# Residual stream turned on VectorE in 32x32 blocks, with block-wise DMAs and a DRAM scratch, instead of by TensorE transposes

## The reference

```
h = rmsnorm(x, norm_mix_g);  z = h @ w_in + b_in      # gates, three mixers A, B, C
mix = sig(ga)*(A @ w_br_a) + sig(gb)*(B @ w_br_b) + sig(gc)*(C @ w_br_c)
x = x + mix @ w_o                                     # first residual sum, "x2"
h2 = rmsnorm(x, norm_ffn_g)
u, v = split(h2 @ w_up);  u = causal_dwconv(u, ffn_conv_w)   # 2816 channels each
x = x + (silu(u) * v) @ w_down                        # second residual sum
return rmsnorm(x, norm_final_g)
```

## Time and profile before

| | |
|---|---|
| three timed runs | 939.05, 939.93, 939.99 us; median 939.93 |
| the profiled execution | 939.24 us, of which span 937.5 us |
| granted PE clock over the span | 0.998 |
| busy | PE 918.0, DVE 495.9, ACT 378.3, POOL 377.4 us |
| DMA | 87.61 MB in 149234 packets, mean 93 GB/s |

### The profile page before, as it was taken

One profiled execution on the slowest core, in us unless ns is written; L12 is line 12 of the kernel. 1 busy time (PEld: TensorE's weight loads), 2 busy tenths in 40 slices (PEclk: granted clock), 3 DMA queues, 4 the chain that ended last, 5 costly groups with the idle time before them and its releaser, 6 DMA issues.

```text
span 937.5 us, 13783 instructions
## 1 busy us (share of the span) xinstructions
PE 918.0 (98%) x4488; PEld 761.0 (81%) x4488; DVE 495.9 (53%) x957; ACT 378.3 (40%) x655; POOL 377.4 (40%) x195
## 2 busy tenths in 40 slices
PE   6999999998999999999999999999999999999997
PEld 5888888887788888888888888888888888888885
DVE  4326464566565645656547687666666666400004
ACT  6445354353444543554533336333333333311125
POOL 4454444442233423324234443444444444444441
PEclk9999999999999999999999999999999999999999
DMA  6353434332122222222253232333333333322232
GB/s 184 94 150 101 108 101 107 105 90 68 46 68 55 81 69 68 70 63 67 67 158 104 76 90 81 99 89 105 97 89 97 105 89 100 124 90 90 90 112 90
DMA packets 149234, 87.61 MB, mean 93 GB/s; under 512 B 24767, under 2 KB 139853, under 8 KB 149205
## 3 DMA queue, kind: packets, MB, share of 16 engines
q1 hardware_dynamic: 149205, 87.23, 32.3%
HBM read 85.09 MB, written 2.11 MB: 93 GB/s over the span
## 4 chain that ended last, share of the span: by engine, by line
PE 94%; DVE 3%; ACT 1%; POOL 1%; DMA 1%; issue 0%; SPq 0%; DVEq 0%; POOLq 0%; ACTq 0%
PE z_bank L647 23%; PE z_bank L649 23%; PE z_bank L648 23%; PE s_bank L647 3%; PE s_bank L648 3%; PE s_bank L649 3%; PE s_bank L683 3%; PE s_bank L703 3%; PE o_bank L722 1%; PE o_bank L647 1%; PE o_bank L723 1%; PE s_bank L723 1%; PE s_bank L722 1%; PE o_bank L649 1%; PE o_bank L648 1%; DMA x_in<-in_x 1%
## 5 line engine op out<-in xcount | busy, mean ns | idle before, releaser
L554 POOL TENSOR_TENSOR w_lo<-raw,w_hi 128x1024 fp32r<-128x1024 f32 (+1 forms) x144 | 352.5, 2448 | 527.1 <-ACT w_hi L967 430.5
L647 PE MATMUL z_bank<-h_hi,w_hi 128*128 128x512 f32 x768 | 302.2, 393 | 0.0
L649 PE MATMUL z_bank<-h_hi,w_lo 128*128 128x512 f32 x768 | 299.6, 390 | 0.0
L648 PE MATMUL z_bank<-h_lo,w_hi 128*128 128x512 f32 x768 | 299.3, 390 | 0.0
L967 ACT ACTIVATE w_hi<-raw 128x1024 fp32r<-128x1024 f32 x117 | 123.4, 1054 | 181.2 <-PE z_bank L649 181.2
L647 PEld LDWEIGHTS z_bank<-h_hi,w_hi 128*128 128x128 f32 x768 | 144.3, 188 | 30.6 <-POOL w_lo L554 0.5
L649 PEld LDWEIGHTS z_bank<-h_hi,w_lo 128*128 128x128 f32 x768 | 144.2, 188 | 30.4
L648 PEld LDWEIGHTS z_bank<-h_lo,w_hi 128*128 128x128 f32 x768 | 144.3, 188 | 28.9
L1570 DVE SCALAR_TENSOR_TENSOR u_c<-u_t,cols,u_c 128x512 f32<-128x512 f32 x44 | 65.8, 1496 | 25.2 <-ACT u_c L1194 22.1
L976 ACT ACTIVATE p_f<-p_f,neg_mx 128x128 f32<-128x128 f32 (+1 forms) x96 | 52.6, 550 | 45.1 <-DVE neg_mx L1438 29.5
L1585 DVE TENSOR_TENSOR y_out<-s_bank,x_t 128x512 f32<-128x512 f32 x5 | 3.5, 691 | 110.4 <-PE s_bank L649 110.3
(11 more groups left out here) (316 smaller groups left out, 1328.3 us busy)
## 6 DMA issues: line engine op xcount, KB each, us to landing
raw<-in_w_in SPq DMA_DIRECT2D x112, 256.0 KB, 3.2
raw<-in_w_up SPq DMA_DIRECT2D x88, 256.0 KB, 3.1
raw<-in_w_down SPq DMA_DIRECT2D x42, 256.0 KB, 2.9
raw<-in_w_o SPq DMA_DIRECT2D x16, 256.0 KB, 3.2
x_in<-in_x SPq DMA_DIRECT2D x4, 512.0 KB, 5.2
f_bias<-cum_scratch SPq DMA_DIRECT2D x4, 512.0 KB, 4.4
raw<-in_w_br_a SPq DMA_DIRECT2D x8, 256.0 KB, 3.0
raw<-in_w_br_b SPq DMA_DIRECT2D x8, 256.0 KB, 3.3
```

The costliest lines, as they stand in the source:

```text
L554: pool.tensor_tensor(w_lo[:, slot, 0:wide], raw[:, slot, 0:wide], w_hi[:, slot, 0:wide].bitcast(F), ALU.subtract) \
L647: pe.matmul(out, w[0], r[0], start=first, stop=False)
L648: pe.matmul(out, w[0], r[1], start=False, stop=False)
L649: return pe.matmul(out, w[1], r[0], start=False, stop=last)
```

## The change

- PE's 32 transposes of `x_r` and 32 of `x2` are gone, with ACT's 8 copies out of PSUM for the first and 8 for the second.
- x is loaded block-wise: four DMAs, each into 32 partitions, each of 4096 pieces of 32 floats (128 B) that stand 512 B apart in DRAM. In `x_b`, partition 32a+j holds, for its 16 tokens, the pieces a of all channel tiles. One DVE instruction per channel tile (`dve.transpose`, on 16 blocks of 32x32) turns them into `x2[:, m, :]`. It reads runs of 32 floats and writes single floats 16 apart.
- After `h_lo`, DVE turns x2 the other way into `x2_b` (single floats 16 apart read, runs of 32 written). SP stores `x2_b` in four DMAs of 4096 pieces of 128 B into a DRAM scratch, behind the loads of UP5, and reads it back as rows in four DMAs of 512 KB into `x2_t`, behind the loads of UP11.
- The squares move from DVE to ACT, between `h_hi` and the next `split_hi`. Their running sum moves from DVE to POOL, behind the `split_lo` of tile m+2.

```diff
@@ buffers
-            x_r = sb("x_r", [P128, QT, D_MODEL], F, s)
+            x_b = sb("x_b", [P128, QT * D_MODEL], F, s)
...
+            x2_b = sb("x2_b", [P128, QT * D_MODEL], F, s)
...
-        x_sq = sb("x_sq", [P128, SEQ], F, ffn)
+        x_sq = sb("x_sq", [P128, 2, SEQ], F, ffn)
@@ SP
-                    for t in range(QT):
-                        sp.dma_start(x_r[:, t, :], x_v[:, t, :]).then_inc(xr_loaded, 16)
+                    by_block = x[0].rearrange("t c -> (t c)").rearrange("(j n a i) -> a j n i", j=BLK, n=P128, a=4)
+                    for a in range(4):
+                        sp.dma_start(x_b[BLK * a:BLK * a + BLK, :].rearrange("p (n i) -> p n i", i=BLK), by_block[a]) \
+                            .then_inc(xb_loaded, 16)
...
-            with sp.Fori(0, FT) as i:
+            for i in range(3):
+                load_up(i)
+            sp.wait_ge(x2_turned, KT)
+            by_block = x2_dram.rearrange("t c -> (t c)").rearrange("(j n a i) -> a j n i", j=BLK, n=P128, a=4)
+            for a in range(4):
+                sp.dma_start(by_block[a], x2_b[BLK * a:BLK * a + BLK, :].rearrange("p (n i) -> p n i", i=BLK)).then_inc(x2_stored, 16)
+            for i in range(3, 6):
+                load_up(i)
+            sp.wait_ge(x2_stored, 16 * 4)
+            for t in range(QT):
+                sp.dma_start(x2_t[:, t, :], x2_dram.rearrange("(t p) n -> p t n", p=P128)[:, t, :]).then_inc(x2_loaded, 16)
+            with sp.Fori(6, FT) as i:
+                load_up(i)
@@ POOL
+            for m in range(KT):
+                split_lo((N_WO + m + 2) % 2, N_WO + m + 2)
+                if m:
+                    pool.wait_ge(sq_done, m + 1)
+                    pool.wait_ge(acc_done, m - 1)
+                    pool.tensor_tensor(x_acc[:, :], x_acc[:, :], x_sq[:, m % 2, :], ALU.add).then_inc(acc_done, 1)
@@ PE
-            pe.wait_ge(xr_loaded, 16 * QT)
             for m in range(KT):
-                if m >= 4:
-                    pe.wait_ge(xr_copied, m - 3)
-                for t in range(QT):
-                    mm = pe.transpose(S[m % 4][:, P128 * t:P128 * t + P128], x_r[:, t, P128 * m:P128 * m + P128], ident[:, :])
-                mm.then_inc(xr_t, 1)
...
-            pe.wait_ge(acc_done, KT)
+            pe.wait_ge(acc_done, KT - 1)
             pe.matmul(S[4][:, :], ones[:, :], x_acc[:, :], start=True, stop=True).then_inc(ss_done, 1)
...
-            pe.wait_ge(xr_copied, KT)
-            turn_x2(0)
             project(0, 1, N_UP + 1, Z_UP[1])
-            pe.wait_ge(x2_kept, QT)
-            turn_x2(1)
@@ ACT
-                act.wait_ge(xr_t, m + 1)
-                act.activation(x2[:, m, :], S[m % 4][:, :], ACT.Copy).then_inc(xr_copied, 1)
...
+                if m > 2:
+                    act.wait_ge(acc_done, m - 2)
+                act.activation(x_sq[:, m % 2, :] if m else x_acc[:, :], x2[:, m, :], ACT.Square).then_inc(sq_done, 1)
@@ DVE
+                if m == 0:
+                    dve.wait_ge(xb_loaded, 16 * 4)
+                dve.transpose(x2[:, m, :].rearrange("p (j b) -> p b j", j=BLK),
+                              x_b[:, :].rearrange("p (b m i) -> p m b i", m=KT, i=BLK)[:, m, :, :]).then_inc(xb_turned, 1)
...
-                sq = x_sq if m else x_acc
-                dve.tensor_tensor(sq[:, :], x2[:, m, :], x2[:, m, :], ALU.mult).then_inc(sq_done if m else acc_done, 1)
-                if m:
-                    dve.wait_ge(sq_done, m)
-                    dve.tensor_tensor(x_acc[:, :], x_acc[:, :], x_sq[:, :], ALU.add).then_inc(acc_done, 1)
+                dve.transpose(x2_b[:, :].rearrange("p (b m i) -> p m b i", m=KT, i=BLK)[:, m, :, :],
+                              x2[:, m, :].rearrange("p (j b) -> p b j", j=BLK)).then_inc(x2_turned, 1)
...
+            dve.wait_ge(x2_loaded, 16 * QT)
```

More of the change, by code:

```diff
@@ L98 @@
 MIX_ORDER = (("gc", 6), ("yc", 0), ("yc", 2), ("gc", 7), ("yc", 4), ("yc", 6))
+BLK = 32
 N_BLK = SEQ // CMP_STRIDE
@@ L255, in hybrid_block @@
         with ExitStack() as s:
-            x_r = sb("x_r", [P128, QT, D_MODEL], F, s)
+            x_b = sb("x_b", [P128, QT * D_MODEL], F, s)
         act_hi = sb("act_hi", [P128, FT, SEQ], R, ffn)
+        with ExitStack() as s:
+            act_lo_ahead = sb("act_lo_ahead", [P128, FT - KT, SEQ], R, s)
+            x2_b = sb("x2_b", [P128, QT * D_MODEL], F, s)
         act_lo = sb("act_lo", [P128, FT, SEQ], R, ffn)
-        x_sq = sb("x_sq", [P128, SEQ], F, ffn)
+        x_sq = sb("x_sq", [P128, 2, SEQ], F, ffn)
         x_acc = sb("x_acc", [P128, SEQ], F, ffn)
@@ L271, in hybrid_block @@
         banks = [*S, O, *Z]
+        x2_dram = nc.dram_tensor("x2_scratch", [SEQ, D_MODEL], F, kind="Internal").ap()
         cum_dram = nc.dram_tensor("cum_scratch", [FOX_HEADS, SEQ], F, kind="Internal").ap()
@@ L330, in hybrid_block @@
         mix_hi = sem("mix_hi"); mix_lo = sem("mix_lo")
-        xr_loaded = sem("xr_loaded"); xr_t = sem("xr_t"); xr_copied = sem("xr_copied");
+        xb_loaded = sem("xb_loaded"); xb_turned = sem("xb_turned")
         xg_hi = sem("xg_hi"); xg_lo = sem("xg_lo"); sq_done = sem("sq_done"); acc_done = sem("acc_done")
@@ L335, in hybrid_block @@
         uv_done = sem("uv_done"); act_hi_done = sem("act_hi_done"); act_lo_done = sem("act_lo_done")
-        down_done = sem("down_done"); x2_turned = sem("x2_turned"); x2_kept = sem("x2_kept")
+        down_done = sem("down_done"); x2_turned = sem("x2_turned"); x2_stored = sem("x2_stored"); x2_loaded = sem("x2_loaded")
         last_loaded = sem("last_loaded"); last_hi_done = sem("last_hi_done"); last_lo_done = sem("last_lo_done")
@@ L521, in _, with load_up @@
                 n += 1
-            with sp.Fori(0, FT) as i:
+            def load_up(i):
                 load8(N_UP + 2 * i, 1, up_k, P128 * i)
                 load8(N_UP + 2 * i + 1, 0, up_k, D_FF + P128 * i)
+            for i in range(3):
[11 more added lines that the diff above has]
+                load_up(i)
             def load_down(n, slot, j):
@@ L634, in _ @@
                                base=SEQ - P128, pattern=[[0, 2], [-1, SEQ]], channel_multiplier=1).then_inc(alibi_ready, 1)
-            with pool.Fori(0, (N_END - 1 - N_NSA - 2) // 2) as i:
+            with pool.Fori(0, (N_WO - N_NSA - 2) // 2) as i:
                 split_lo(1, N_NSA + 2 * i + 2)
                 split_lo(0, N_NSA + 2 * i + 3)
+            split_lo(N_WO % 2, N_WO)
+            split_lo((N_WO + 1) % 2, N_WO + 1)
+            for m in range(KT):
[4 more added lines that the diff above has]
+                    pool.tensor_tensor(x_acc[:, :], x_acc[:, :], x_sq[:, m % 2, :], ALU.add).then_inc(acc_done, 1)
+            with pool.Fori(0, (N_END - 1 - N_UP - 2) // 2) as i:
+                split_lo(1, N_UP + 2 * i + 2)
+                split_lo(0, N_UP + 2 * i + 3)
             pool.wait_ge(last_hi_done, 1)
@@ L926, in down @@
                 return mm3(banks[2 * t + h][:, :], (act_hi[:, j, toks], act_lo[:, j, toks]), (whi[:, cols], wlo[:, cols]), first, last)
-            pe.wait_ge(x2_kept, 2 * QT)
             for j in range(FT - 2):
@@ L1179, in _ @@
             act.activation(rstd[:, :], S[4][:, :], ACT.Sqrt, bias=eps_c[:, :], scale=1.0 / D_MODEL).then_inc(rs_sqrt, 1)
[L1181 to L1186, removed]
             act.activation(act_cell[:, 3:4], eps_c[:, :], ACT.Silu)
@@ L1199, in up_pair @@
                 act.activation(act_hi[:, i, :], u_c[:, :], ACT.Copy).then_inc(act_hi_done, 1)
-            up_pair(0)
-            keep_x2(1)
-            with act.Fori(1, FT) as i:
+            with act.Fori(0, FT) as i:
                 up_pair(i)
@@ L1541, in _ @@
                 z = m % 2
-                dve.wait_ge(xr_copied, m + 1)
+                if m == 0:
+                    dve.wait_ge(xb_loaded, 16 * 4)
+                dve.transpose(x2[:, m, :].rearrange("p (j b) -> p b j", j=BLK),
+                              x_b[:, :].rearrange("p (b m i) -> p m b i", m=KT, i=BLK)[:, m, :, :]).then_inc(xb_turned, 1)
+                dve.wait_ge(xb_turned, m + 1)
                 dve.wait_ge(tile_done, T_WO + m + 1)
@@ L1548, in _ @@
                                          ALU.mult, ALU.subtract).then_inc(xg_lo, 1)
-                if m:
-                    dve.wait_ge(acc_done, m)
-                sq = x_sq if m else x_acc
-                dve.tensor_tensor(sq[:, :], x2[:, m, :], x2[:, m, :], ALU.mult).then_inc(sq_done if m else acc_done, 1)
-                if m:
-                    dve.wait_ge(sq_done, m)
-                    dve.tensor_tensor(x_acc[:, :], x_acc[:, :], x_sq[:, :], ALU.add).then_inc(acc_done, 1)
+                dve.transpose(x2_b[:, :].rearrange("p (b m i) -> p m b i", m=KT, i=BLK)[:, m, :, :],
+                              x2[:, m, :].rearrange("p (j b) -> p b j", j=BLK)).then_inc(x2_turned, 1)
             dve.memset(u_t[:, 0:2], 0.0).then_inc(rs_ready, 1)
```

## The result

| | before | after |
|---|---|---|
| median, us | 939.49 (938.67 to 939.99, 4 runs) | 959.93 (958.9 to 961.02, 4 runs) |
| profiled execution, us | 939.24 | 958.9 |
| its span, us | 937.5 | 957.2 |
| mean granted clock of TensorE | 0.998 | 0.987 |

After is slower by 2.2%: the ratio is 1.022, with an interval of 1.0206 to 1.0233. The forecast was 941.1 in a range of 936 to 952, so the time lies outside it, on the side that the forecast called the likelier.

The account below looks back on a forecast made before the run. PE was taken as the bound, 94% of the chain that ended last. From the profiled 939.24: minus 3.8 won on PE, plus 1.3 for the load of x, plus 4.4 for the store of x2, gives 941.1 us; range 936 to 952.

Parts of the forecast that it names:

- what leaves PE: Transposes gone from the WO tiles and behind the ones matmul: 6.8 us taken off PE, 3.8 us won in all.
- T: Start of the ones matmul, from which later tiles are counted; predicted at 567.7, against 569.12 before.
- The two DVE instructions that I took at 1.5: Ahead of the first pair's silu, before UP3's weight split: 1.5 us predicted with POOL idle, against 2.90 before.
- rival 5: DVE becomes the bound in the WO tiles if a transpose takes 2.78 us: 17 us lost, 958; chance 0.08.
- I take 11.5, between the line and the count: Load of x: ns per 128 B packet, between 9.4 (line through 256 and 512 B) and 14.1 (packets alone count).
- rival 3: Block transfers: packets count, 12.7 to 14.1 ns each or a little more, 943.5 to 947 us; chance 0.17.
- Rival 4: Store of x2: 128 B writes to DRAM cost double, S = 23.6, stall at UP6 16.2 us, 952.9; chance 0.15.
- X: Duration of the block load of x ahead of gc 7's weights: 11.8 us predicted (9.6 to 14.4).
- S: Duration of the block store of x2 ahead of UP6's weights: 11.8 us predicted, costing 4.4 us (2.2 to 7.0).
- landing must be by 494.2: X up to 10.5 costs nothing: gc 7's weights, wanted at 498.05 less the splits' 1.14 + 2.54; X = 11.8 costs 1.3 us (0 to 3.9).
- 483.7 + X: Predicted landing of gc 7's weights: issue at 480.87, 0.9 and 0.4 us of delays, 1.5 us for 512 KB, plus X.
- the formula: At UP6: weights land at T+18.2+S, due at T+25.6, so 7.4 us are free; S = 11.8 costs 4.4 us.

Follow-up runs that it names:

- Run 9: Changed kernel with both block transfers in 4 KB pieces, each DMA over all 128 partitions instead of 32; 936.02 us, ratio 0.9963 to the kernel before.
- run 11: Changed kernel with both block transfers in 256 B pieces, each DMA over all 128 partitions instead of 32; 945.65 us, ratio 1.0073 to the kernel before.
- run 4: Changed kernel with ACT's two copies to `br_hi` ahead of the split of the next weights in the branch steps, instead of behind it; 956.79 us.
- run 6: Changed kernel with both block transfers in 4 KB pieces instead of 128 B, still 32 partitions per DMA; 950.20 us.
- run 12: Changed kernel with both block transfers in 4 KB pieces, each DMA over 64 partitions; 946.93 us, ratio 1.0088 to the kernel before.
- run 10: Changed kernel, pieces still 128 B, but each DMA over all 128 partitions instead of 32; 959.11 us, ratio 1.021 to the kernel before.
- run 3: Changed kernel with block loads spread over three places of SP's program and one weight load behind each block store; 937.29 us, ratio 0.9978 to the kernel before.

## Why the prediction was wrong

**Right in mechanism and nearly in size: what leaves PE.** From the first matmul of WO0 to the ones matmul are 53.36 us, against 54.31 before: 0.95 won, 1.4 predicted. UP2 starts at T+6.84 (6.75 predicted), UP3 at T+13.18 (12.95). The two DVE instructions that I took at 1.5 took 0.75 each with POOL idle. In all 3.1 us, 3.8 predicted. Run 9, where both transfers are fast, has a span of 934.5, 3.0 below 937.5: the gain is there when nothing is lost. The transposes took 1.05 and 1.08 us (1.3 predicted, no cost up to 1.6), so rival 5 is out.

**The step that failed first: "I take 11.5, between the line and the count".** A packet costs 13.9 ns. This was rival 3, and rows 4 spoke for it: packets of 256 B at 14.1 ns. At 128 B the count came nearest, and in part by luck: in the shape of these transfers 256 B cost not the same but 18.9 ns (run 11), and 64 B 11.8. The Trainium skill, DMA: Bandwidth & Descriptors, "Why small descriptors are slow", gave an estimate of 9.0 ns by its 3 cycles; the traces do not agree. Rival 4, the doubled writes, is out: the store ran at the load's rate. The time of a read-modify-write, which the Trainium skill, DMA: Bandwidth & Descriptors, "Specifications", has below 512 B, shows in no row.

**But the right price would not have been enough.** By my own formulas X = S = 14.3 costs 3.8 us at gc 7 and 6.9 at UP6, 946.1 in all, 5.0 above the forecast. The profiled execution took 958.9. The other 12.8 us are:

- *gc 7, 5.4 us*, the larger failed step: "landing must be by 494.2: X up to 10.5 costs nothing" took the splits as the only thing behind the landing. 3.8 us is the copies that stand behind the blocked split on ACT, shown by run 4: 1.8 us of slack that the chain over `br_hi`, `br_lo` and `g_c` did not leave even before, and 1.9 us by which `br_lo` got longer. I had named no instruction that queues behind the waiting one, and ACT's rows of before had it: `br_hi` right behind `w_hi`. 1.6 us is data later than 483.7 + X = 498.0: `w_hi` starts 3.3 us behind the last packet of x, where the sum has 1.9. SP, held by the block DMAs, issued the weights only from 491.47 to 495.58, but that is not needed for it: in run 6, where they were issued from 486.95 to 487.89, `w_hi` starts 3.4 us behind the last packet too, in run 12 2.5. Why they land so late stays open.
- *UP6, 2.0 us*: 8.9 where the formula gives 6.9. The path was right: UP5's load was issued at T+13.1, the store behind it at T+14.1. The store lasted 16.4 us in place of 14.3, mostly by its three dips, and with S = 16.4 the formula gives 9.0. In run 10 the store took 14.5 us, for which it gives 7.1, and PE waits 7.15 there.
- *The slow matmuls, 4.5 us* (2.8 + 1.7). The sum put what the clock takes after a wait at nothing. Before had no idle of this length in this stretch, and so no row of it.
- *The gain, 0.7 us smaller.*

These are 12.6. **Why so many losses at once**: each needs a wait longer than the slack. Where the order on SP is changed (run 3), nearly all of them go together (1.1 us stays at gc 7), at an unchanged price of the packet. The forecast argued about a price within 2 ns, while the place of the eight DMAs in one queue decided over 22 us.

What stays open: why SP's issue of each block DMA after the first takes 3.0 to 4.8 us. The four loads take 10.92 us with 4096 pieces each, 10.75 with as many over 128 partitions (run 10), and 2.56 with 128 pieces each (run 6). So it goes above all with the number of pieces; what is full then no row shows. Also not tried: both DMAs of a pair in flight on different halves of the partitions.

## What to carry to other kernels

Price a DMA by its pieces and by the partitions that it touches, each by itself, and then ask what stands behind it in the queue: spreading eight block DMAs between the weight loads gained 22.6 us (959.93 to 937.29) where their price did not change. When a wait is found too long for its slack, list every instruction behind the waiting one on the same engine and who needs it, and add what the clock takes after an idle of this length. Instructions of a finished tile go ahead of one that waits for data.

## What the hardware showed unexpectedly

- SP is held by a DMA of 4096 pieces: the first is issued in 0.65 us, the others take 3.0 to 4.8 us each, which is the pace of the transfer; a load in 4 KB pieces is issued in 0.44 (run 9) to 0.64 us (run 6).
- After 9.3 and 8.9 us without a matmul, TensorE's granted clock was 0.50 (1.2 GHz) for about 6 and 3 us of matmuls; after 7.4 us (run 4) for 2.7 us. It fell during the idle: 1.00 in the first 4.8 us ahead of gc 7, 0.53 in the next 4.5. The span lost 4.5 us by it.
- Packets of 128 B cost 14 ns per DMA engine, to DRAM as from it (14.5 and 14.4 us for 2 MB in run 10); packets of 64 B 11.8 ns. Halving the piece again saves only 2 ns per packet.
- Transfers of 4 KB pieces on 32 or 64 partitions moved about 200 GB/s (runs 6 and 12), on 128 355 to 437 (run 9).
- DVE's `br_lo`, with two sources, took 0.74 us with POOL idle (508.96, two in 1.48) and 2.6 us beside POOL's `w_lo` (501.24, two in 5.16).
